# Two projection tiles started over the first 256 tokens ahead of the last token block's turn, the gate's product behind it

## The chip, the cores and the metric

The kernel runs on one core of a Trainium2 chip. The metric is the device time of one execution in microseconds; the kernel before took 1502.77 us as the median of three runs (1499.66 to 1587.22). The engines that matter here are TensorE (PE, with its weight loads PEld), VectorE (DVE), ScalarE (ACT), GpSimd (POOL) and SyncE (SP), whose queue issues the weight transfers.

## The reference

The reference is a decoder trunk of two layers over one sequence of 512 tokens with 1024 channels. Layer 0 mixes tokens with a gated DeltaNet, layer 1 with sparse attention; each is followed by a SwiGLU. What matters here is how one sublayer hands over to the next:

```python
y = gdn_mixer(h, ...)                  # or dsa_mixer, or swiglu: ends in a product with w_out
x = x + (1.0 + ga_m) * rms_norm(y, norm_g[layer, 1])
h = rms_norm(x, norm_g[layer, 2]) * (1.0 + sc_f) + sh_f
gate, up = jnp.split(h @ ffn_w_in[layer], 2, axis=-1)   # the next projection
```

Both norms are over the 1024 channels of one token, so a token's h exists only when its whole y does.

## The kernel before, in words

**Layout.** The 512 tokens are four blocks of 128. The stream x (`x_t`) and each sublayer's output y have tokens on the partitions; the projections want h with channels on the partitions. Between them x is turned on TensorE: a product of 128 x 128 of x with a diagonal matrix that holds 1/rms of each token (`diag`), which transposes and normalizes at once. ACT and DVE then apply scale and shift and cut h into two float32r parts, `h_hi` (rounded) and `h_lo` (the rest). Weights are cut in the same way: ACT makes `w_hi` from the raw weights (`act_split`, L368), DVE makes `w_lo` (`dve_split`, L383). A product is then three: hi x hi, hi x lo, lo x hi.

**Quads and tiles.** Weights come in quads of four tiles (s = 0 to 3) of 128 output channels by 1024 input channels. Tile s is accumulated in PSUM bank s over all 512 tokens, in 8 steps k of 128 channels, 24 products of 512 columns in all (`pe_tile`, L387). SP loads the raw weights of the next quad in two halves (`load_quad`, L330); each half waits until the low parts of two tiles of the quad before are made (`lo_done`). `hi_done` and `lo_done` count split tiles, `tile_done` counts tiles that TensorE has finished.

**The seams.** There are four output stages `pe_out` / `act_out` / `dve_out` / `pool_out` with m = 0 to 3 (DeltaNet's output, the first SwiGLU's, the attention's, the second SwiGLU's). For m = 0, 1 and 2 a projection follows: the first SwiGLU's, the attention's (`dsa_in_pe`), the second SwiGLU's (`ffn_pe`). Such a handover is called a seam here. At its end, for the last block b = 3 (`end`), one chain passes all engines:

- `pe_out` makes y of the block, then turns the block before it (`pe_turn_x`, L693);
- ACT squares y (L794) and DVE scales it by the gate `CB[m]` (L838), adds up the row sum (L841), GpSimd raises it to the power -1/2 (L911, the first root), DVE updates x (L851);
- ACT squares x (L805), DVE adds up (L856), GpSimd takes the second root (L916), DVE makes `diag` (L861);
- TensorE turns the block (L700) into banks 4 to 7, in two groups g of four chunks;
- for the last block ACT writes `h_hi` of group 0 directly from PSUM (`h_last`, L760), DVE writes `h_raw` of group 1, then of group 0 (`h_scale`, L867), ACT rounds group 1 (L766), and DVE makes `h_lo` (`h_low`, L878).

DVE's order after the last block's y is in `dve_out`: split of tile 0 under the first root, `h_scale` of group 1 of block 2 after x, `h_low` of block 2 around the second root, split of tile 1, then the last block's h.

TensorE's first tile of the next quad is `pe_behind_out` (L401): the products with `h_hi` first, as ACT rounds the two groups (`h_rounded`), then those with `h_lo` (`h_made`). Tiles 1 to 3 are plain `pe_tile`.

**The gate's product.** `pe_cb` (L657) multiplies a matrix of ones with a diagonal gate, four products of f32, to spread the gate over all partitions; ACT copies the result into `CB` (`act_cb`, L665). For m = 1 and 2 it stands in TensorE's queue between the turn of block 2 and the turn of block 3 and uses banks 0 and 1. Each engine runs its own instructions in the order written; only semaphores order them against each other.

Of the kernel before, what the change touches and what calls it, by code (L numbers as in the profile page):

```python
# [19 lines left out]
P = 128  # L20
# [58 lines left out]
def build_trunk(nc, x, c, ada_w, ada_b, norm_g, ffn_w_in, ffn_w_out,  # L79
# [4 lines left out]
    DC = D // P  # L84
    NB = S // P
# [19 lines left out]
    Q_FFN = [Q_GDN_OUT + 2, 0]  # L105
# [5 lines left out]
    with ExitStack() as ctx:  # L111
# [178 lines left out]
        def sem(name):  # L290
            if name not in sems:
                sems[name] = ctx.enter_context(nc.semaphore(name))
            return sems[name]
# [13 lines left out]
        def split_tile(w, s, kc=8):  # L307
            return w[:, s, 0:kc * P].rearrange("p (k n) -> p k n", n=P)
# [89 lines left out]
                last = nc.tensor.matmul(out_, lo[:, k, :], r_hi[:, k, :], start=False, stop=k == kc - 1)  # L398
            last.then_inc(tile_done, 1)

        def pe_behind_out(pe, q, m):  # L401

            h = OUT_H[m]
            pe.wait_ge(lo_done, q * 4 + 1)
            hi, lo = split_tile(w_hi, 0), split_tile(w_lo, 0)
            for k in range(DC):
                pe.wait_ge(sem("h_rounded"), 8 * h + 7 + (k >= 4))
                nc.tensor.matmul(ps[:, 0, :], hi[:, k, :], h_hi[:, k, :], start=k == 0, stop=False)
                nc.tensor.matmul(ps[:, 0, :], lo[:, k, :], h_hi[:, k, :], start=False, stop=False)
            for k in range(DC):  # L410
                pe.wait_ge(sem("h_made"), 8 * h + 7 + (k >= 4))
                last = nc.tensor.matmul(ps[:, 0, :], hi[:, k, :], h_lo[:, k, :], start=False, stop=k == DC - 1)
            last.then_inc(tile_done, 1)

        def pe_first_quad(pe, q, r_hi, r_lo, ready, before=None, after=None, between=None):

# [246 lines left out]
            last.then_inc(sem("h_mm"), 1)  # L663

        def act_cb(act, m, bank0):  # L665
            act.wait_ge(sem("h_mm"), DC + 1 if m == 0 else turn_no(m - 1, 3, 1) + 1 if m == 1 else turn_no(m - 1, 2, 1) + 1)
            for j in range(2):
                nc.scalar.activation(CB[m][:, j * S:(j + 1) * S], ps[:, bank0 + j, :], ACT.Copy)\
                    .then_inc(sem("cb_out"), 1)
# [12 lines left out]

        def turn_no(m, b, g):

            return DC + 1 + 9 * m + 2 * b + g + 1 + (1 if m and b == NB - 1 else 0)

        Y_MM = [0, 20, 28, 48]

# [18 lines left out]
        def pe_out(pe, m, q, kc, s_hi, s_lo, ready=None, free=None):  # L707

            late = LATE[m]
            for b in range(NB):  # L710
                if b >= 2 and m % 2:
                    pe.wait_ge(sem("y_added"), 8 * (m // 2) + 2 * (b - 2) + 2)
                elif b >= 2:
                    pe.wait_ge(sem("row_sq"), sq_no(m, b - 2, 0) + 2)
                    pe.wait_ge(sem("y_scaled"), 8 * m + 2 * (b - 2) + 2)
                elif free:
                    free(b)

                def product(k, j):
                    hi, lo = (w_hi[:, k, :], w_lo[:, k, :]) if k < 4 else (late[0][:, k - 4, :], late[1][:, k - 4, :])  # L720
                    cols, toks, to = slice(j * S, (j + 1) * S), slice(b * P, (b + 1) * P), 2 * (b % 2) + j
                    nc.tensor.matmul(ps[:, to, :], s_hi[:, k, toks], hi[:, cols], start=k == 0, stop=False)  # L722
                    nc.tensor.matmul(ps[:, to, :], s_hi[:, k, toks], lo[:, cols], start=False, stop=False)  # L723
                    return nc.tensor.matmul(ps[:, to, :], s_lo[:, k, toks], hi[:, cols], start=False, stop=k == kc - 1)  # L724

                for k in range(4):
                    if b == 0:
                        pe.wait_ge(lo_done, 4 * q + k + 1)
                        if ready:
                            ready(k)  # L730
                    if m == 0 and k == 0:
                        gdn_out_ready(pe, b, k)
                    for j in range(2):
                        last = product(k, j)
                    if b == NB - 1:
                        last.then_inc(tile_done, 1)
                for j in range(2):
                    for k in range(4, kc):
                        if b == 0:
                            per = 4 // (kc - 4)  # L740
                            pe.wait_ge(lo_done, 4 * q + 4 + (k - 4) * per + (per if per == 1 else j + 1))
                            if ready and j == 0:
                                ready(k)
                        if m == 0 and j == 0 and k == 4:
                            gdn_out_ready(pe, b, k)
                        last = product(k, j)
                    last.then_inc(sem("y_mm"), 1)
                if b and m < 3:
                    pe_turn_x(pe, m, b - 1)
            if 1 <= m < 3:  # L750
                pe_cb(pe, m + 1, 0)
            if m < 3:
                pe_turn_x(pe, m, NB - 1)

        def act_out(act, m, nxt):

# [30 lines left out]
            for b in range(NB):  # L787
# [18 lines left out]
                                         accum_out=row_stat[:, 1, b, j:j + 1]).then_inc(sem("row_sq"), 1)  # L806
                if b == NB - 1:
                    h_second(b - 1)
                if m and b == NB - 1:
                    act_cb(act, m + 1, 0)  # L810
                if b == 2:
                    nxt(0)
                    nxt(1)
            if m < 3:
                h_last(NB - 1)
                nxt(2)
                nxt(3)

        def dve_out(dve, m, nxt):
# [31 lines left out]
                    nc.vector.scalar_tensor_tensor(x_half, tmp[:, j, :], row_rinv[:, 0, b:b + 1], x_half,  # L851
                                                   ALU.mult, ALU.add).then_inc(sem("x_made"), 1)

            def root(b, meanwhile=None):
                dve.wait_ge(sem("row_sq"), sq_no(m, b, 1) + 2)
                nc.vector.scalar_tensor_tensor(row_var[:, 1, b:b + 1], row_stat[:, 1, b, 0:1], EPS,  # L856
                                               row_stat[:, 1, b, 1:2], ALU.add, ALU.add).then_inc(sem("row_made"), 1)
                if meanwhile:
                    meanwhile()
                dve.wait_ge(sem("row_root"), row(m, b, 1) + 2)  # L860
                nc.vector.tensor_scalar(diag[:, b, :], ident[:, :], row_rinv[:, 1, b:b + 1], None, ALU.mult)\  # L861
                    .then_inc(sem("x_diag"), 1)
# [28 lines left out]
            if m == 3:  # L891
                scaled(end)
                return
            scaled(end, lambda: nxt(0))
            h_scale(end - 1, 1)
            root(end, lambda: h_low(end - 1, 0))
            h_low(end - 1, 1)
            nxt(1)
            h_scale(end, 1)
            dve.wait_ge(sem("h_rounded"), 8 * OUT_H[m] + 2 * end + 1)  # L900
            h_scale(end, 0)
            h_low(end, 0)
            h_low(end, 1)
            nxt(2)
# [1034 lines left out]
        def ffn_pe(pe, layer, m):  # L1939
            for p in range(3):  # L1940
# [3 lines left out]
                def body(i):  # L1944
                    for s in range(4):
# [7 lines left out]
                            else:  # L1953
                                pe.wait_ge(sem("ffn_silu" if s < 2 else "ffn_mul"), (i + c0) * 2 - 1 + s % 2)

                        if start and s == 0:
                            pe_behind_out(pe, q, 2 * layer)
                        else:
                            pe_tile(pe, i + q, s, h_hi, h_lo, before=free)
                        if layer == 0 and s == 0 and not start:  # L1960
# [105 lines left out]
        def dsa_in_pe(pe, m):  # L2066
            for s in range(4):
                if s == 0:
                    pe_behind_out(pe, Q_DSA, 1)
                else:  # L2070
                    pe_tile(pe, Q_DSA, s, h_hi, h_lo)
                if s == 2:
                    pe_stats(pe, 0, sq_lat[:, 0, :, :], LC)
# [618 lines left out]
```

## Time and profile before

| | |
|---|---|
| median of 3 runs | 1502.77 us (1499.66 to 1587.22) |
| the profiled execution | 1500.31 us |
| its span, first to last instruction | 1498.7 us |
| mean granted TensorE clock | 0.961 |
| TensorE busy | 1385.4 us, 92% |
| VectorE busy | 850.5 us, 57% |
| ScalarE busy | 531.8 us, 35% |
| GpSimd busy | 151.0 us, 10% |

The table is read from the top: the span is what the profiler saw, the time is a little longer than it. The granted clock is the share of 2.4 GHz that TensorE was given. TensorE carries the kernel; the products of the projections (lines 396 to 398) alone are 2808 instructions.

### The profile page before, as it was taken

What the parts mean: (1) busy time and instruction counts of PE and PEld (TensorE: products, weight loads), DVE (VectorE), ACT (ScalarE), POOL (GpSimd) and SP (SyncE); (2) the same over time, 40 slices, a digit from 0 to 9 for tenths busy, and PEclk for the clock granted to TensorE, in tenths of its full rate; (3) what the DMA queues carried; (4) which work ended last, traced back from release to release, by engine and by line L of the source; (5) the groups of instructions that cost most, each with busy time, mean ns of one, the idle gap of its engine ahead of it and who ended that gap; (6) DMA issues with size and microseconds to landing.
All of it is one profiled execution on the core that took longest, in us unless ns stands there. A gap on an engine that the chain in (4) does not pass through costs nothing. (4 is left out here: it accounts for less than half of the span.)

```text
span 1498.7 us, 17980 instructions
## 1 busy us (share of the span) xinstructions
PE 1385.4 (92%) x6983; PEld 1116.6 (75%) x6983; DVE 850.5 (57%) x1412; ACT 531.8 (35%) x953; POOL 151.0 (10%) x155
## 2 busy tenths in 40 slices
PE   5798899899989999999999887699989999999998
PEld 5676777779778878887888765556778888888886
DVE  4768799746555555555555649956453332332335
ACT  2353522345452212221224525476253221221322
POOL 0003330003410000000000102300010000000000
PEclk9899999899999999999999988899999999999999
DMA  9453412110404546455532120200102313322321
GB/s 329 155 169 112 165 61 85 46 68 1 169 28 144 202 159 197 168 168 177 187 141 84 51 56 29 68 18 2 57 29 90 107 61 119 102 84 84 112 84 57
DMA packets 102854, 158.37 MB, mean 106 GB/s; under 512 B 9325, under 2 KB 74106, under 8 KB 102778
## 3 DMA queue, kind: packets, MB, share of 16 engines
q1 hardware_dynamic: 91898, 115.40, 23.5%
q0 software_dynamic: 10880, 41.95, 8.1%
q8 instruction: 49, 0.80, 0.2%
q14 instruction: 27, 0.22, 0.1%
HBM read 155.24 MB, written 2.10 MB: 105 GB/s over the span
## 5 line engine op out<-in xcount | busy, mean ns | idle before, releaser
L396 PE MATMUL ps<-h_hi,w_hi 128*128 128x512 f32 x936 | 378.4, 404 | 0.0
L397 PE MATMUL ps<-h_lo,w_hi 128*128 128x512 f32 x936 | 372.3, 398 | 0.0
L398 PE MATMUL ps<-h_hi,w_lo 128*128 128x512 f32 x936 | 372.3, 398 | 0.0
L380 DVE TENSOR_TENSOR w_lo<-raw,w_hi 128x1024 fp32r<-128x1024 f32 x172 | 210.7, 1232 | 250.1 <-ACT w_hi L374 249.8
L374 ACT ACTIVATE w_hi<-raw 128x1024 fp32r<-128x1024 f32 x180 | 187.7, 1050 | 150.9 <-PE ps L1994 143.0
L396 PEld LDWEIGHTS ps<-h_hi,w_hi 128*128 128x128 f32 x936 | 178.6, 191 | 42.6 <-issue 1.7
L397 PEld LDWEIGHTS ps<-h_lo,w_hi 128*128 128x128 f32 x936 | 178.4, 191 | 42.7 <-issue 1.7
L398 PEld LDWEIGHTS ps<-h_hi,w_lo 128*128 128x128 f32 x936 | 177.8, 190 | 42.5
L462 DVE SCALAR_TENSOR_TENSOR ada_acc<-ada_in,c_act,ada_acc 128x512 f32<-128x512 f32 x147 | 112.9, 768 | 3.9
L1992 PE MATMUL ps<-w_hi,g_hi 128*128 128x512 f32 x256 | 101.6, 397 | 2.6 <-DVE w_lo L380 2.6
L1857 ACT ACTIVATE g_hi<-tmp 128x512 fp32r<-128x512 f32 x44 | 27.8, 632 | 212.0 <-DVE tmp L1892 212.0
L1994 PE MATMUL ps<-w_hi,g_lo 128*128 128x512 f32 x256 | 101.0, 395 | 0.0
L1993 PE MATMUL ps<-w_lo,g_hi 128*128 128x512 f32 x256 | 101.0, 395 | 0.0
L995 DVE SCALAR_TENSOR_TENSOR tmp<-conv_u,conv_t,tmp 128x512 f32<-128x512 f32 x72 | 59.6, 827 | 38.5 <-ACT tmp L989 36.4
L1852 ACT ACTIVATE silu_g<-ps 128x512 f32<-128x512 f32 x44 | 26.3, 597 | 154.1 <-PE ps L398 150.3
L911 POOL TENSOR_TENSOR row_rinv<-row_var,half 128x1 f32<-128x1 f32 x16 | 11.5, 716 | 576.6 <-DVE row_var L841 576.6
L361 POOL DMA_DIRECT2D ada_in<-in_ada_w_dram x40 | 30.5, 761 | 374.5 <-DVE ada_acc L462 365.5
L1892 DVE TENSOR_TENSOR tmp<-silu_g,ps 128x512 f32<-128x512 f32 x44 | 30.3, 688 | 63.5 <-PE ps L398 63.1
L1992 PEld LDWEIGHTS ps<-w_hi,g_hi 128*128 128x128 f32 x256 | 48.1, 188 | 14.7 <-DVE w_lo L380 3.4
L1994 PEld LDWEIGHTS ps<-w_hi,g_lo 128*128 128x128 f32 x256 | 48.1, 188 | 11.5
L1993 PEld LDWEIGHTS ps<-w_lo,g_hi 128*128 128x128 f32 x256 | 48.2, 188 | 11.2
L2441 DVE CUSTOM_DVE_ANT_0 s_m<-ps,mask 128x128 f32<-128x128 f32 (+3 forms) x64 | 29.0, 488 | 26.0 <-PE ps L2341 25.7
(374 smaller groups left out, 2073.3 us busy)
## 6 DMA issues: line engine op xcount, KB each, us to landing
raw<-in_ffn_w_in_dram SPq DMA_DIRECT2D x44, 1024.0 KB, 5.1
ada_in<-in_ada_w_dram POOLq DMA_DIRECT2D x40, 1024.0 KB, 5.7
raw<-in_ffn_w_out_dram SPq DMA_DIRECT2D x20, 1024.0 KB, 5.0
raw<-in_gdn_w_in_dram SPq DMA_DIRECT2D x16, 1024.0 KB, 5.7
ada_in<-in_ada_w_dram SPq DMA_DIRECT2D x4, 1024.0 KB, 7.2
x_t<-in_x_dram SPq DMA_DIRECT2D x2, 2048.0 KB, 9.7
early_slab<-in_ada_w_dram SPq DMA_DIRECT2D x4, 1024.0 KB, 12.3
raw<-in_gdn_w_out_dram SPq DMA_DIRECT2D x4, 1024.0 KB, 4.9
```

Source lines behind the costliest of these rows:

```text
L361: sp.dma_start(slab_place(j)[b][:, :, :], src[b][:, :, bass.ds(jj * 512, 512)])\
L374: nc.scalar.activation(split_tile(w_hi, s, kc) if dst is None else dst(w_hi), raw_tile(s, kc) if src is None else src, ACT.Copy).then_inc( ...
L380: ops.tensor_tensor(lo, raw_tile(s, kc) if src is None else src, f32(hi), ALU.subtract).then_inc(lo_done, 1)
L396: nc.tensor.matmul(out_, hi[:, k, :], r_hi[:, k, :], start=k == 0, stop=False)
L397: nc.tensor.matmul(out_, hi[:, k, :], r_lo[:, k, :], start=False, stop=False)
L398: last = nc.tensor.matmul(out_, lo[:, k, :], r_hi[:, k, :], start=False, stop=k == kc - 1)
L462: ins = nc.vector.scalar_tensor_tensor(ada_acc[:, :], slab_place(j)[b][:, k, :], cc, ada_acc[:, :], ALU.mult, ALU.add)
L995: ins = nc.vector.scalar_tensor_tensor(conv_a[n % 2], conv_u[n % 2][:, j:j + S], conv_t[:, j, channel(n):channel(n) + 1], conv_a[n % 2], A ...
L1892: nc.vector.tensor_tensor(gated[:, s - 2, :], silu_g[:, s - 2, :], ps[:, s, :], ALU.mult)\
L1992: nc.tensor.matmul(ps[:, b, :], g_hi[:, k, toks], hi, start=k == 0, stop=False)
L1993: nc.tensor.matmul(ps[:, b, :], g_hi[:, k, toks], lo, start=False, stop=False)
L1994: last = nc.tensor.matmul(ps[:, b, :], g_lo[:, k, toks], hi, start=False, stop=k == PARTS[p] - 1)
```

## The change

The first tile's function `pe_behind_out` is replaced by two functions that treat tiles 0 and 1 together and split the tokens. `pe_first_tokens` runs the products of `w_hi` with `h_hi` and `h_lo` over tokens 0 to 255; it is called before the last block's turn. `pe_last_tokens` runs, after the turn, the same over tokens 256 to 511, and the products of `w_lo` over all 512. The gate's product moves behind the last turn and from banks 0 and 1 to banks 2 and 3, and ACT's copies of it move behind `h_last`. On DVE, `h_scale` of block 2 moves under the first root, where the split of tile 0 stood; nothing is put under the second root; the split of tile 0 comes after `diag` and that of tile 1 after the last block's `h_scale`. `turn_no` follows the new order of TensorE's signals.

```diff
--- before.py
+++ after.py
@@ -398,19 +398,41 @@
                 last = nc.tensor.matmul(out_, lo[:, k, :], r_hi[:, k, :], start=False, stop=k == kc - 1)
             last.then_inc(tile_done, 1)
 
-        def pe_behind_out(pe, q, m):
-
-            h = OUT_H[m]
-            pe.wait_ge(lo_done, q * 4 + 1)
-            hi, lo = split_tile(w_hi, 0), split_tile(w_lo, 0)
-            for k in range(DC):
-                pe.wait_ge(sem("h_rounded"), 8 * h + 7 + (k >= 4))
-                nc.tensor.matmul(ps[:, 0, :], hi[:, k, :], h_hi[:, k, :], start=k == 0, stop=False)
-                nc.tensor.matmul(ps[:, 0, :], lo[:, k, :], h_hi[:, k, :], start=False, stop=False)
-            for k in range(DC):
-                pe.wait_ge(sem("h_made"), 8 * h + 7 + (k >= 4))
-                last = nc.tensor.matmul(ps[:, 0, :], hi[:, k, :], h_lo[:, k, :], start=False, stop=k == DC - 1)
-            last.then_inc(tile_done, 1)
+        def pe_first_tokens(pe, q):
+
+            part = slice(0, 2 * P)
+            for s in range(2):
+                pe.wait_ge(hi_done, q * 4 + s + 1)
+                hi = split_tile(w_hi, s)
+                for k in range(DC):
+                    nc.tensor.matmul(ps[:, s, part], hi[:, k, :], h_hi[:, k, part], start=k == 0, stop=False,
+                                     skip_group_check=True)
+                    nc.tensor.matmul(ps[:, s, part], hi[:, k, :], h_lo[:, k, part], start=False, stop=False,
+                                     skip_group_check=True)
+
+        def pe_last_tokens(pe, q, m):
+
+            part, h = slice(2 * P, 4 * P), OUT_H[m]
+            for s in range(2):
+                pe.wait_ge(lo_done, q * 4 + s + 1)
+                hi, lo = split_tile(w_hi, s), split_tile(w_lo, s)
+                for k in range(DC):
+                    if s == 0:
+                        pe.wait_ge(sem("h_rounded"), 8 * h + 7 + (k >= 4))
+                    nc.tensor.matmul(ps[:, s, part], hi[:, k, :], h_hi[:, k, part], start=False, stop=False,
+                                     skip_group_check=True)
+                    if k < DC - 1:
+                        nc.tensor.matmul(ps[:, s, :], lo[:, k, :], h_hi[:, k, :], start=False, stop=False,
+                                         skip_group_check=True)
+            for s in range(2):
+                hi, lo = split_tile(w_hi, s), split_tile(w_lo, s)
+                for k in range(DC):
+                    if s == 0:
+                        pe.wait_ge(sem("h_made"), 8 * h + 7 + (k >= 4))
+                    nc.tensor.matmul(ps[:, s, part], hi[:, k, :], h_lo[:, k, part], start=False, stop=False,
+                                     skip_group_check=True)
+                nc.tensor.matmul(ps[:, s, :], lo[:, DC - 1, :], h_hi[:, DC - 1, :], start=False, stop=True,
+                                 skip_group_check=True).then_inc(tile_done, 1)
 
         def pe_first_quad(pe, q, r_hi, r_lo, ready, before=None, after=None, between=None):
 
@@ -663,7 +685,7 @@
             last.then_inc(sem("h_mm"), 1)
 
         def act_cb(act, m, bank0):
-            act.wait_ge(sem("h_mm"), DC + 1 if m == 0 else turn_no(m - 1, 3, 1) + 1 if m == 1 else turn_no(m - 1, 2, 1) + 1)
+            act.wait_ge(sem("h_mm"), DC + 1 if m == 0 else turn_no(m - 1, 3, 1) + 1)
             for j in range(2):
                 nc.scalar.activation(CB[m][:, j * S:(j + 1) * S], ps[:, bank0 + j, :], ACT.Copy)\
                     .then_inc(sem("cb_out"), 1)
@@ -682,7 +704,7 @@
 
         def turn_no(m, b, g):
 
-            return DC + 1 + 9 * m + 2 * b + g + 1 + (1 if m and b == NB - 1 else 0)
+            return DC + 1 + 9 * m + 2 * b + g + 1
 
         Y_MM = [0, 20, 28, 48]
 
@@ -747,10 +769,11 @@
                     last.then_inc(sem("y_mm"), 1)
                 if b and m < 3:
                     pe_turn_x(pe, m, b - 1)
+            if m < 3:
+                pe_first_tokens(pe, (Q_FFN[0], Q_DSA, Q_FFN[1])[m])
+                pe_turn_x(pe, m, NB - 1)
             if 1 <= m < 3:
-                pe_cb(pe, m + 1, 0)
-            if m < 3:
-                pe_turn_x(pe, m, NB - 1)
+                pe_cb(pe, m + 1, 2)
 
         def act_out(act, m, nxt):
 
@@ -806,13 +829,13 @@
                                          accum_out=row_stat[:, 1, b, j:j + 1]).then_inc(sem("row_sq"), 1)
                 if b == NB - 1:
                     h_second(b - 1)
-                if m and b == NB - 1:
-                    act_cb(act, m + 1, 0)
                 if b == 2:
                     nxt(0)
                     nxt(1)
             if m < 3:
                 h_last(NB - 1)
+                if m:
+                    act_cb(act, m + 1, 2)
                 nxt(2)
                 nxt(3)
 
@@ -851,12 +874,10 @@
                     nc.vector.scalar_tensor_tensor(x_half, tmp[:, j, :], row_rinv[:, 0, b:b + 1], x_half,
                                                    ALU.mult, ALU.add).then_inc(sem("x_made"), 1)
 
-            def root(b, meanwhile=None):
+            def root(b):
                 dve.wait_ge(sem("row_sq"), sq_no(m, b, 1) + 2)
                 nc.vector.scalar_tensor_tensor(row_var[:, 1, b:b + 1], row_stat[:, 1, b, 0:1], EPS,
                                                row_stat[:, 1, b, 1:2], ALU.add, ALU.add).then_inc(sem("row_made"), 1)
-                if meanwhile:
-                    meanwhile()
                 dve.wait_ge(sem("row_root"), row(m, b, 1) + 2)
                 nc.vector.tensor_scalar(diag[:, b, :], ident[:, :], row_rinv[:, 1, b:b + 1], None, ALU.mult)\
                     .then_inc(sem("x_diag"), 1)
@@ -891,14 +912,15 @@
             if m == 3:
                 scaled(end)
                 return
-            scaled(end, lambda: nxt(0))
-            h_scale(end - 1, 1)
-            root(end, lambda: h_low(end - 1, 0))
-            h_low(end - 1, 1)
-            nxt(1)
+            scaled(end, lambda: h_scale(end - 1, 1))
+            root(end)
+            nxt(0)
+            h_low(end - 1, 0)
             h_scale(end, 1)
             dve.wait_ge(sem("h_rounded"), 8 * OUT_H[m] + 2 * end + 1)
             h_scale(end, 0)
+            nxt(1)
+            h_low(end - 1, 1)
             h_low(end, 0)
             h_low(end, 1)
             nxt(2)
@@ -1953,8 +1975,9 @@
                             else:
                                 pe.wait_ge(sem("ffn_silu" if s < 2 else "ffn_mul"), (i + c0) * 2 - 1 + s % 2)
 
-                        if start and s == 0:
-                            pe_behind_out(pe, q, 2 * layer)
+                        if start and s < 2:
+                            if s == 0:
+                                pe_last_tokens(pe, q, 2 * layer)
                         else:
                             pe_tile(pe, i + q, s, h_hi, h_lo, before=free)
                         if layer == 0 and s == 0 and not start:
@@ -2066,8 +2089,8 @@
         def dsa_in_pe(pe, m):
             for s in range(4):
                 if s == 0:
-                    pe_behind_out(pe, Q_DSA, 1)
-                else:
+                    pe_last_tokens(pe, Q_DSA, 1)
+                elif s >= 2:
                     pe_tile(pe, Q_DSA, s, h_hi, h_lo)
                 if s == 2:
                     pe_stats(pe, 0, sq_lat[:, 0, :, :], LC)
```

## Rows read from the trace of the kernel before

**Rows 1.** The page, part 1: busy us (share of the span), instructions.

```profile
PE 1385.4 (92%) x6983; PEld 1116.6 (75%) x6983; DVE 850.5 (57%) x1412; ACT 531.8 (35%) x953; POOL 151.0 (10%) x155
```

**Rows 2.** Waits of TensorE: total us, times, longest.

```profile
PE ps L700 <- issue: 13.5, 3, 5.5
```

**Rows 3.** Busy time in four stretches, first seam: each engine, granted clock, DMA.

```profile
437.93:443.42 5.49, 0.01 (x1) 0.04 (x1) 4.62 (x11) 3.35 (x8) 2.19 (x2) 0.79 0.00 0
443.42:447.15 3.73, 3.73 (x17) 3.48 (x17) 1.63 (x2) 1.50 (x4) 0.00 (x0) 0.50 0.22 43
447.15:453.15 6.00, 6.00 (x25) 4.87 (x25) 5.84 (x12) 2.54 (x3) 0.00 (x0) 0.94 0.43 150
453.15:458.70 5.55, 5.55 (x25) 4.53 (x24) 2.74 (x4) 1.55 (x2) 0.00 (x0) 1.00 0.56 189
```

**Rows 4.** The same view, second and third seam: turn of the last block.

```profile
844.48:848.18 3.70, 3.36 (x16) 3.17 (x16) 1.93 (x3) 1.65 (x5) 0.00 (x0) 0.62 0.25 48
1117.74:1121.45 3.71, 3.71 (x16) 3.46 (x17) 1.64 (x2) 1.66 (x5) 0.00 (x0) 0.50 0.13 35
```

**Rows 5.** Timeline of TensorE: start, us; first matmul of each seam's third tile.

```profile
458.74 0.39 PE L396 MATMUL ps<-h_hi,w_hi 128*128 128x512 f32 x1
...
859.48 0.39 PE L396 MATMUL ps<-h_hi,w_hi 128*128 128x512 f32 x1
...
1133.79 0.40 PE L396 MATMUL ps<-h_hi,w_hi 128*128 128x512 f32 x1
```

**Rows 6.** Timeline of all engines, first seam, from the third block's turn.

```profile
435.98 1.95 PE L700 MATMUL ps<-diag,x_t 128*128 128x128 f32 x16
...
439.23 1.41 DVE L851 SCALAR_TENSOR_TENSOR x_t<-tmp,row_rinv,x_t 128x512 f32<-128x512 f32 x2 [0.44 <-POOL row_rinv L911]
...
440.56 1.36 DVE L867 TENSOR_SCALAR h_raw<-ps,coef,mod 128x128 f32<-128x128 f32 x4
...
441.36 0.19 ACT L805 ACTIVATION_READ_ACCUMULATOR tmp<-x_t 128x1 f32 x1
441.84 0.15 DVE L856 SCALAR_TENSOR_TENSOR row_var<-row_stat 128x1 f32<-128x1 f32 x1
...
442.07 0.93 POOL L916 TENSOR_TENSOR row_rinv<-row_var,half 128x1 f32<-128x1 f32 x1 [2.87 <-DVE row_var L856]
443.03 0.29 DVE L861 TENSOR_SCALAR diag<-ident,row_rinv 128x128 f32<-128x128 f32 x1 [0.44 <-POOL row_rinv L916]
...
443.42 3.75 PE L700 MATMUL ps<-diag,x_t 128*128 128x128 f32 x16 [5.49 <-issue]
443.83 1.22 DVE L380 TENSOR_TENSOR w_lo<-raw,w_hi 128x1024 fp32r<-128x1024 f32 x1
...
445.50 1.50 ACT L760 ACTIVATE h_hi<-ps,mod,coef 128x128 fp32r<-128x128 f32 x4 [2.91 <-PE ps L700]
...
447.15 0.77 PE L408 MATMUL ps<-h_hi,w_hi 128*128 128x512 f32 x1
```

**Rows 7.** Timeline, second seam (three rows) and third seam (one row).

```profile
840.29 1.41 DVE L851 SCALAR_TENSOR_TENSOR x_t<-tmp,row_rinv,x_t 128x512 f32<-128x512 f32 x2 [0.44 <-POOL row_rinv L911]
...
842.90 0.15 DVE L856 SCALAR_TENSOR_TENSOR row_var<-row_stat 128x1 f32<-128x1 f32 x1
...
844.48 1.84 PE L700 MATMUL ps<-diag,x_t 128*128 128x128 f32 x7 [4.25 <-issue]
...
1112.10 1.88 PE L662 MATMUL ps<-p_t,ones 128*128 128x512 f32 x4
```

**Rows 8.** Line 911 (GpSimd's first root): ns min/median/max.

```profile
L911 POOL TENSOR_TENSOR row_rinv<-row_var,half x16: 537/541/1457, 404.1 to 1494.3; 128x1 f32<-128x1 f32 x16
```

**Rows 9.** Line 700's weight loads: ns min/median/max.

```profile
L700 PEld LDWEIGHTS ps<-diag,x_t x192: 187/192/338, 410.0 to 1120.9; 128*128 128x128 f32 x192
```

**Rows 10.** Timeline of TensorE: eight one-column products.

```profile
116.17 0.95 PE L1023 MATMUL ps<-ones,tmp 128*128 128x1 f32 x8
```

**Rows 11.** DMA issues, 440 to 470 us: KB each, median us to landing.

```profile
raw<-in_ffn_w_in_dram SPq DMA_DIRECT2D x3, 1024.0 KB, 5.2
```

## The prediction

> **What bounds the kernel now.** I read the share of busy time first: TensorE is busy for 92% of the span [rows 1], so time can only be won where TensorE stands still or runs at its lower clock. The view of waits, asked for TensorE, then names where: line 700, the turn of x, sat behind 13.5 us of idle time in three waits [rows 2]. Those are the three seams the diff touches (m = 0, 1, 2), where the last token block must pass ACT, DVE, GpSimd and the turn before the next projection can begin.
>
> The stretches of the first seam show what one costs. TensorE idles 5.49 us; the granted clock falls, and the turn of the last block runs at 0.50 of full clock (1.2 instead of 2.4 GHz), 3.73 us; tiles 0 and 1 then take 6.00 and 5.55 us [rows 3]. The same 16 products took 1.95 us for the third block at full clock [rows 6]. The last turn is slow in the other seams too (3.70 us at 0.62, 3.71 us at 0.50) [rows 4]. The timeline shows the chain behind the idle time: x updated, both halves squared, the row sum (L856) held until four h_scale instructions end, GpSimd's root at 0.93 us, diag, the turn, ACT's h_hi, first product [rows 6].
>
> **What a half-width product costs.** The change splits the 48 products of 512 columns of tiles 0 and 1 into 64 of 256 columns and 16 of 512. No row has a 256-column product of this kind. A 512-column one costs 5.55 us / 24 = 0.231 us [rows 3]. A turn product (128 columns, f32) costs 1.95/16 = 0.122 us with a weight load of its own [rows 6]; a one-column product costs (0.95 - 0.25)/7 = 0.10 us, 0.25 being an estimated tail [rows 10], so the load alone allows 0.10. Bounds: half of the full product, 0.115, below; the full product's 0.231 above. I take 0.123, next to the turn product, which has just as small a body and as many loads. Columns and thus array work are unchanged; the extra is 64 x (0.123 - 0.1155), 0.5 us in a seam.
>
> **The first tokens in the gap.** 32 half products are 3.94 us. They need the third turn, blocks 0 and 1 of h, and the high halves of two weight tiles that ACT split while the last block was computed; none is late. In seam one they run from 437.93 to 441.87 us. They lie wholly in the gap.
>
> **The chain to the last turn.** DVE does h_scale where it did a split (1.22 us [rows 6]), under the first root. Four h_scale instructions hold DVE for 1.28 us and can start when the third turn ends, 437.97; x would be updated at 439.25 instead of 439.23. So nothing is won there. Afterwards no h_scale stands before L856: it follows ACT's second accumulator read, which ended at 441.55 [rows 6], at 441.59 instead of 441.84. Then the root: 0.93 us of GpSimd with h_low beside it, against a median of 0.541 for the same tiny operation, whose worst was 1.457 [rows 6, 8]. With DVE idle beside it I take 0.54: another 0.38 won. The turn begins at 443.42 - 0.25 - 0.38 = 442.8. TensorE idles 0.9 us instead of 5.5, too little for the clock to fall as it did (the stretch of 5.49 us still averaged 0.79 [rows 3]), and the turn takes 1.95 us, to 444.75.
>
> The trace shows the root slow beside a two-input DVE operation on SBUF. The Trainium skill (SBUF — State Buffer, "SBUF: two separate sides") says the shared port pair is an exclusive lock between DVE with two SBUF inputs and GpSimd; a PSUM-reading h_scale would not take it. By that rule the roots take 0.54; without it they keep 1.46 and 0.93, and the three turns come 0.4 to 0.7 us later.
>
> **The last tokens.** At half clock h_hi began 2.08 us after the turn; at full clock I scale it to 1.08, so 443.9, and the first product follows 1.65 us after [rows 6]: 445.5. Tile 0's part: 8 x (0.123 + 0.231) - 0.231 = 2.60 us, to 448.1. Its second half needs h_rounded of the second group, 446.9, just in time. Tile 1 waits for its low split (lo_done). DVE's new queue is: diag 442.4, split 0 to 443.85, h_low to 444.5, h_scale of the last block after the turn, eight instructions to 447.35, then split 1, to 448.6. TensorE waits 0.6 us. Tile 1's part ends at 451.3, the low parts of h cost 2 x (8 x 0.123 + 0.231) = 2.43 us: 453.75. h_low of the last block ends at 450.6, in time. Before, the third tile began at 458.74 [rows 5]. **Seam one: 5.0 us won.**
>
> **Seam two.** Here split 0 sat before x's update at 840.29 and the third turn was over earlier, so h_scale lets x be updated at 839.92, 0.37 earlier; L856 goes from 842.90 to 842.27 [rows 7], the root saves 0.38: turn at 843.47 instead of 844.48, to 845.42. The first tokens fill 838.5 to 842.45. The gate's product (pe_cb, four products, 1.88 us with its tail [rows 7], 1.72 of cadence) used to lie in the gap for nothing; now it stands behind the turn, and the last tokens can begin at 847.15 rather than 846.2: 0.95 us of it is paid. Split 1 ends at 849.3, no wait. 847.15 + 2.60 + 2.60 + 2.43 = 854.8 against 859.48 [rows 5]: **4.7 us.** ACT's copies of the gate now delay splits 2 and 3 by 1.1 us; split 2's low half is there by 852.5, 2 us before tile 2 wants it.
>
> **Seam three.** As seam one for the chain: turn 1117.74 - 0.62 = 1117.1 to 1119.1, the gate's product to 1120.8, then 7.63 us: 1128.4 against 1133.79 [rows 5]: **5.4 us**, more because the clock had stayed low into tile 0.
>
> **Moved past a queue.** SP loads the next weight pair when split 1 is done. That moves from 445.05 to 448.6 us, 3.6 later; the load lands 5.2 us on [rows 11], 453.8, where ACT wants it at about 453.3. TensorE wants that tile at 453.75 + 11.1 = 464.9, so 0.5 us of ACT delay is covered by some 9 us. GpSimd's queue has only the roots here, now earlier. DVE's other moves are order alone.
>
> **Sum.** 5.0 + 4.7 + 5.4 = 15.1 us. Downstream everything follows TensorE, so I take all of it. Against the profiled execution (1500.31 us, span 1498.7) that is 1485.2. Its time is 2.5 us under the median of the runs shown (1502.77), whose lowest is 1499.66; 1502.77 - 15.1 would be 1487.7. I say 1486.
>
> **Rivals.**
> - *Gain given back (0.15).* The shortened seams meet a new wait: tile 1 on its split in all seams, or the attention layer's first stages, which wait for DVE and ACT chains rather than TensorE. Against it: only one of three seams shows a 0.6 us wait in my sum. If a third to two thirds is lost: 1490 to 1495.
> - *The load is not hidden (0.07), the slower side.* Each half product pays its weight load before it streams 0.107 us. With the load at its recorded 0.19 us [rows 9] it takes 0.30: 64 x 0.177 = 11.3 us in a seam beyond my sum, of which the 0.9 of idle and the 0.6 of wait absorb 1.5; 9.8 - 5.0 = 4.8 us lost in each, 1500.3 + 14.4 = 1515 (0.04). With the load at the 0.10 of the one-column products [rows 10] it takes 0.207: 64 x 0.084 - 1.5 = 3.9 us of each seam's 5.0 are gone, 1497 (0.03). It turns from gain to loss at 0.123 + 6.5/64 = 0.225 us per half product. Against it: turn products, each with a load, run at 0.122 [rows 6].
> - *The whole waste goes (0.05).* TensorE never waits: seam one alone holds 20.8 us from 437.93 to 458.74 for 13.5 us of work, three such gaps about 22 us in all: 1478. It would need the diag to come a microsecond sooner and the last h_hi chain (2.7 us from turn to first product) to vanish; I see no cover for the latter.
> - *The split does nothing (0.02)*: the clock falls all the same in the remaining gap, since 32 small products are thinner work. Then turn and start cost their old 2.5 us again: 1493.
>
> The Trainium skill speaks for that rival (TensorE: Matmul & The Clock Gate, "What overlaps and what doesn't"): a weight load overlaps a running product only when their row groups differ, which no product here does. This trace doesn't agree: full products, each with its own load, follow every 0.231 us, of which 512 columns at 2.4 GHz fill 0.213. By the page's load time of P/1.2, an estimate of 0.107 us, a half product would cost 0.214 and the gain would shrink to about 2 us.
>
> **Chances.** Forecast 0.71, rivals 0.15, 0.07, 0.05, 0.02. The forecast's own range is 1482 to 1490 (half product 0.115 to 0.14, roots 0.54 or slow, which median it is held against). Stretched to the first rival, the clock's and the cheaper load's: 1480 to 1497, which leaves out the 0.04, the 0.05 and the edges of the forecast. A measurement of this kernel tells about 2%, 30 us, from no change. All waste of the three seams is under that, so faster by over 2% gets 0.02; slower by over 2% would need 0.30 us products twice over, 0.02; within 2%: 0.96.
>
> **What would show it.** In the changed trace: 32 products of 256 columns at 0.12 us each in front of the last turn; idle before line 700 about 1 us, three times; granted clock 1.0 through the turn, 1.95 us each; GpSimd's last two roots at 0.54; about 0.6 us of wait before tile 1 in seam one, none in the other two; the next load's issue 3.5 us later with no wait of TensorE for w_lo in the next pair. The prediction is wrong if half products run at over 0.15 us, if the turn stays at 3.7 us, or if the attention layer's waits grow by what the second seam wins.

## The result and the profile after

The changed kernel took 1483.21 us as the median of four runs (1481.28 to 1486.83) against 1501.97 of four for the kernel before; the ratio is 0.9883, 95% interval 0.9856 to 0.991. One execution of the kernel before was in a slower state (1587.22 us) and is left out of the ratio. The forecast was 1486 with 1480 to 1497. A second series of the same kernel on another occasion gave 0.9909 (0.9894 to 0.9924), so the gain is about 18 us by the first series and 14 by the second. The profiled execution took 1483.27 us, its span is 1481.6 us, 17.1 less than before.

The page's part 1 (busy us, share, instructions) and the view of waits of TensorE (total, times, longest), which answer to [rows 1, 2]:

```profile
PE 1373.8 (93%) x7079; PEld 1111.9 (75%) x7079; DVE 850.4 (57%) x1412; ACT 531.3 (36%) x953; POOL 147.6 (10%) x155
```

```profile
PE ps L722 <- issue: 3.3, 3, 1.2
...
PE ps L422 <- ACT h_hi L783: 0.8, 1, 0.8
...
PE ps L422 <- DVE w_lo L380: 0.3, 1, 0.3
```

The turn (now line 722) waits 3.3 us in three seams where it waited 13.5; 96 more products are issued and TensorE is busy 11.6 us less, because fewer of its products run at half clock (mean granted clock 0.971, before 0.961). The stretches of seam one (columns as in [rows 3]: length, busy time of PE, PEld, DVE, ACT, POOL, granted clock, DMA) and the last turn of seams two and three, which answer to [rows 3, 4]:

```profile
439.28:443.08 3.80, 3.80 (x33) 3.59 (x31) 2.82 (x7) 2.89 (x8) 0.35 (x1) 1.00 0.00 0
443.08:444.16 1.08, 0.00 (x0) 0.03 (x1) 0.42 (x3) 0.36 (x1) 0.54 (x1) 1.00 0.00 0
444.16:446.18 2.02, 2.02 (x16) 1.83 (x16) 1.63 (x2) 0.85 (x3) 0.00 (x0) 1.00 0.00 0
446.18:455.09 8.91, 7.85 (x49) 6.96 (x49) 7.85 (x14) 3.78 (x6) 0.00 (x0) 1.00 0.36 120
839.85:841.87 2.02, 2.02 (x17) 2.02 (x18) 1.63 (x2) 0.86 (x3) 0.00 (x0) 1.00 0.00 0
1105.96:1107.98 2.02, 2.02 (x17) 2.02 (x18) 1.64 (x2) 0.85 (x3) 0.00 (x0) 1.00 0.00 0
```

The gap of 5.49 us holds 3.80 us of products and 1.08 of idle time, and the clock is at 1.00 (2.4 GHz) from end to end. The timeline of seam one shows the chain, row by row against [rows 6]:

```profile
439.24 0.28 PE L410 MATMUL ps<-h_lo,w_hi 128*128 128x256 f32 x1
...
440.61 1.41 DVE L874 SCALAR_TENSOR_TENSOR x_t<-tmp,row_rinv,x_t 128x512 f32<-128x512 f32 x2
...
442.80 0.28 PE L410 MATMUL ps<-h_lo,w_hi 128*128 128x256 f32 x1
...
442.96 0.16 DVE L879 SCALAR_TENSOR_TENSOR row_var<-row_stat 128x1 f32<-128x1 f32 x1 [0.94 <-ACT tmp L828]
443.19 0.54 POOL L938 TENSOR_TENSOR row_rinv<-row_var,half 128x1 f32<-128x1 f32 x1 [3.56 <-DVE row_var L879]
443.77 0.28 DVE L882 TENSOR_SCALAR diag<-ident,row_rinv 128x128 f32<-128x128 f32 x1 [0.66 <-POOL row_rinv L938]
...
444.16 2.02 PE L722 MATMUL ps<-diag,x_t 128*128 128x128 f32 x16 [1.08 <-issue]
...
446.98 0.36 PE L422 MATMUL ps<-h_hi,w_hi 128*128 128x256 f32 x1 [0.80 <-ACT h_hi L783]
...
448.78 1.22 DVE L380 TENSOR_TENSOR w_lo<-raw,w_hi 128x1024 fp32r<-128x1024 f32 x1
...
450.05 0.39 PE L422 MATMUL ps<-h_hi,w_hi 128*128 128x256 f32 x1 [0.26 <-DVE w_lo L380]
```

The third tile's first product, in the three seams, against [rows 5]:

```profile
455.09 0.39 PE L396 MATMUL ps<-h_hi,w_hi 128*128 128x512 f32 x1
...
850.92 0.39 PE L396 MATMUL ps<-h_hi,w_hi 128*128 128x512 f32 x1
...
1117.06 0.39 PE L396 MATMUL ps<-h_hi,w_hi 128*128 128x512 f32 x1
```

**Where the 17.1 us are.** I cut each trace at the end of the third turn and at the third tile's first product of each seam. "Seam" below is the stretch between the two:

| trace | seam 1 | seam 2 | seam 3 | their sum | between 2 and 3 |
|---|---|---|---|---|---|
| before | 20.8 | 21.0 | 21.5 | 63.3 | 252.8 |
| changed | 15.8 | 16.0 | 16.0 | 47.8 | 250.2 |

The seams give 15.5 us. The stage between seams two and three, whose code is the same, gives 2.6; the stretch ahead of seam one took 1.4 us more, what follows seam three 0.3 less. The 1.4 us are not the change's either: when the changed kernel ran once more, that stretch took 437.3 us, against 439.3 here and 437.9 before. The difference lies in waits for VectorE inside DeltaNet (`qkv` 6.8 us against 5.2 in the kernel before and in the repeat, `w_quarter` 4.8 against 3.2). The stage between seams one and two is equal (379.8 in both).

### The profile page after: what moved, and what is told of

Its sections match the earlier page's. It is cut to its first block and busy times, and to the rows that moved or that the text cites. A ratio compares the mean times of both kernels' runs of the same rounds, so it can differ in the third digit from the quotient of the medians.

```text
span 1481.6 us, 18172 instructions
## 1 busy us (share of the span) xinstructions
PE 1373.8 (93%) x7079; PEld 1111.9 (75%) x7079; DVE 850.4 (57%) x1412; ACT 531.3 (36%) x953; POOL 147.6 (10%) x155
## 5 line engine op out<-in xcount | busy, mean ns | idle before, releaser
L396 PE MATMUL ps<-h_hi,w_hi 128*128 128x512 f32 x912 | 367.7, 403 | 0.0
L397 PE MATMUL ps<-h_lo,w_hi 128*128 128x512 f32 x912 | 361.6, 396 | 0.0
L398 PE MATMUL ps<-h_hi,w_lo 128*128 128x512 f32 x912 | 361.4, 396 | 0.0
L397 PEld LDWEIGHTS ps<-h_lo,w_hi 128*128 128x128 f32 x912 | 173.3, 190 | 41.1 <-issue 1.7
L396 PEld LDWEIGHTS ps<-h_hi,w_hi 128*128 128x128 f32 x912 | 173.3, 190 | 41.0 <-issue 1.7
L398 PEld LDWEIGHTS ps<-h_hi,w_lo 128*128 128x128 f32 x912 | 172.7, 189 | 41.0
```

Source lines behind the costliest of these rows:

```text
L396: nc.tensor.matmul(out_, hi[:, k, :], r_hi[:, k, :], start=k == 0, stop=False)
L397: nc.tensor.matmul(out_, hi[:, k, :], r_lo[:, k, :], start=False, stop=False)
```

## The experiments

Each was compared with the kernel before on the same chip. The first four take the change apart.

**DVE's new order alone.** The kernel before with:

```diff
-            scaled(end, lambda: nxt(0))
-            h_scale(end - 1, 1)
-            root(end, lambda: h_low(end - 1, 0))
-            h_low(end - 1, 1)
-            nxt(1)
+            scaled(end, lambda: h_scale(end - 1, 1))
+            root(end)
+            nxt(0)
+            h_low(end - 1, 0)
             h_scale(end, 1)
             dve.wait_ge(sem("h_rounded"), 8 * OUT_H[m] + 2 * end + 1)
             h_scale(end, 0)
+            nxt(1)
+            h_low(end - 1, 1)
             h_low(end, 0)
```

> The kernel before with DVE's new order alone. TensorE's order is the old one, with no work in the gap. My theory (the gain is TensorE's idle time and its low clock): the last turn starts 0.6, 1.0 and 0.6 us sooner in the three seams, its clock still falls, so the stretch from the end of the third turn to the third tile goes from 20.8, 21.0 and 21.5 us to about 20.2, 20.0 and 20.9: 2.2 us won, 0.15%. Rival (DVE's order, with the free port under the roots, is what pays): 5 us or more won, and a turn at full clock.

Measured: ratio 0.9982 (0.9969 to 0.9995). Seams of 21.2, 21.2 and 19.5 us: 1.4 won in all, not 2.2, and spread otherwise than I said. TensorE's rows with idle time, in seams one, two and three:

```profile
442.65 3.75 PE L700 MATMUL ps<-diag,x_t 128*128 128x128 f32 x16 [4.87 <-issue]
451.47 2.13 PE L412 MATMUL ps<-h_lo,w_hi 128*128 128x512 f32 x8 [0.47 <-DVE h_lo L878]
...
843.74 3.65 PE L700 MATMUL ps<-diag,x_t 128*128 128x128 f32 x16 [3.24 <-issue]
...
852.46 2.12 PE L412 MATMUL ps<-h_lo,w_hi 128*128 128x512 f32 x8 [0.81 <-DVE h_lo L878]
...
1115.04 2.02 PE L700 MATMUL ps<-diag,x_t 128*128 128x128 f32 x16 [3.15 <-issue]
```

The idle time shrinks by the forecast 0.6 to 1.0 us. But the old TensorE order then waits for DVE, which has put the split of tile 1 ahead of h_low: 0.47 us of idle time in seam one, 0.81 in seam two and 0.32 in seam three. I had not counted that wait. With it seam one is 0.4 us longer where it should have won 0.6, and seam two 0.2 us longer where it should have won 1.0. In seam three the turn ran at full clock after 3.15 us of idle time, in seam two at half after 3.24; the 2.0 us won in seam three are mostly the clock's. The rival, 5 us or more from DVE's order, is out.

**TensorE's new order alone.** The changed kernel with the hunk above undone; `root` again takes work to do under the root.

> The changed kernel with DVE's old order: splits of tiles 0 and 1 and h_low under the roots. TensorE's new order and the gate's product behind the turn stay. My theory: each last turn starts 0.6, 1.0 and 0.6 us later than in the changed kernel, tile 1's wait for its split in seam one goes, so 2.0 us are lost of the 17: stretches of 16.2, 17.0 and 16.6 us against 15.8, 16.0 and 16.0, about 1485 us. Rival (DVE's order is what pays): 5 us or more lost; GpSimd's last two roots are slow again (0.9 to 1.5 us) in both.

Measured: 0.9922 (0.9898 to 0.9945); seams 15.9, 18.7 and 16.6, together 3.3 us more than the changed kernel against 2.0 expected. Seams one and three came as I said or better; seam two lost 2.7 and not 1.0. Its stretches, idle and turn:

```profile
837.96:840.14 2.18, 0.00 (x1) 0.03 (x1) 1.74 (x7) 0.95 (x3) 0.93 (x1) 1.00 0.00 0
840.14:843.10 2.96, 2.96 (x17) 2.96 (x18) 1.64 (x2) 1.51 (x4) 0.00 (x0) 0.65 0.05 8
```

A gap of 2.18 us leaves the clock at 1.00 within the gap and at 0.65 over the turn behind it, and the gate's product started at half clock too. The turn began 1.0 us later than in the changed kernel (5.97 us behind the third turn's end, against 4.97), as expected; the other 1.7 us of seam two's loss come behind its start and go with the lower clock. So of the 3.3 us that DVE's order is worth, about 1.6 are its timing and 1.7 the clock that a smaller gap kept. GpSimd's roots are slow again (line 934 is the first root; ns min/median/max), against 0.59 at most in the changed kernel (line 933):

```profile
L934 POOL TENSOR_TENSOR row_rinv<-row_var,half x16: 538/542/1457, 404.7 to 1480.5; 128x1 f32<-128x1 f32 x16
```

```profile
L933 POOL TENSOR_TENSOR row_rinv<-row_var,half x16: 540/540/585, 405.5 to 1477.2; 128x1 f32<-128x1 f32 x16
```

**The clock by itself.** The kernel before with unused products ahead of the last turn:

```diff
+                pe.wait_ge(sem("y_scaled"), 8 * m + 2 * (NB - 1) + 2)
+                pe.wait_ge(sem("row_sq"), sq_no(m, NB - 1, 0) + 2)
+                for s in range(2):
+                    pe.wait_ge(hi_done, (Q_FFN[0], Q_DSA, Q_FFN[1])[m] * 4 + s + 1)
+                    for k in range(DC if m == 0 else 6):
+                        for part_of in (h_hi, h_lo):
+                            nc.tensor.matmul(ps[:, 2 + s, 0:2 * P], split_tile(w_hi, s)[:, k, :],
+                                             part_of[:, k, 0:2 * P], start=k == 0, stop=False,
+                                             skip_group_check=True)
                 pe_turn_x(pe, m, NB - 1)
```

> The kernel before with work that nobody uses in the gap ahead of the last turn: 32 (seam one) and 24 (seams two and three) products of 256 columns into banks 2 and 3, which are overwritten later. Nothing is moved. It takes the clock by itself. My theory: the turn runs at full clock (1.95 us), h_hi begins 1.1 us after it and not 2.1, tile 0 starts at full clock: 1.45, 1.1 and 2.0 us won in the seams, 4.6 in all, about 1496 us; the rest of the 15.5 is the work moved into the gap. Rival (the clock costs nothing that counts, h_hi's chain sets it all): no change within 1 us.

Measured: 0.9964 (0.9953 to 0.9975); seams 19.5, 20.0 and 19.5, 4.2 us won where 4.6 were expected. Seam one:

```profile
445.91 2.02 PE L700 MATMUL ps<-diag,x_t 128*128 128x128 f32 x16 [1.69 <-issue]
448.72 0.47 PE L408 MATMUL ps<-h_hi,w_hi 128*128 128x512 f32 x1 [0.80 <-ACT h_hi L769]
```

Of the 1.7 us that the turn is shorter, 0.80 comes back as a wait for ACT's h_hi; 0.3 us more are won in tile 0, which starts at full clock. In all the clock pays 1.3, 1.0 and 2.0 us in the three seams. The rest of the gain, 15.5 - 4.2 = 11.3 us, is close to three times the 3.80 us of first tokens, which are now useful work. That it is so close is partly chance, as smaller terms nearly cancel: the turns begin 0.6, 1.0 and 0.6 us sooner, and against that stand the gate's product (0.75 us, twice) and tile 1's wait (0.4 us).

**The first tokens behind the turn.** The changed kernel with two lines exchanged:

```diff
-                pe_first_tokens(pe, (Q_FFN[0], Q_DSA, Q_FFN[1])[m])
                 pe_turn_x(pe, m, NB - 1)
+                pe_first_tokens(pe, (Q_FFN[0], Q_DSA, Q_FFN[1])[m])
```

> The changed kernel with the first tokens' products behind the last turn and not ahead of it; same products, same DVE order. My theory (their place is what pays, not the split of the tiles): TensorE idles 4.9 us again in each seam, the turn takes about 3.7, the first tokens 4 to 6 us behind it, where they cover only the 0.8 us wait for h_hi; stretches of about 21, 23 and 23 us, 1500 to 1504 us in all, no better than before. Rival (two tiles treated together pay by themselves, since the chain of h_hi and h_lo is covered by them wherever they stand): 8 us or more of the 17 remain.

Measured: 0.9995 (0.9984 to 1.0006); seams 20.5, 21.8 and 22.3, in all 1.2 us longer than before. All turns are back at half clock; seam one:

```profile
443.42 3.75 PE L722 MATMUL ps<-diag,x_t 128*128 128x128 f32 x16 [4.87 <-issue]
```

Seams two and three also carry the gate's product behind the turn here (1.7 us), which the kernel before had in the gap. Seam one has none and is the clean comparison: 20.5 us against 20.8. So the same products in the same number, with DVE's new order, win 0.3 us behind the turn, where the changed kernel wins 5.0 with them ahead of it. Their place is what pays.

**The changed kernel and the kernel before once more**, for the size and for the stage between seams two and three.

> The changed kernel once more, unaltered, beside the others on one chip. Settles the size and what of the 17 us lies outside the seams. My theory: the three stretches come out at 15.8, 16.0 and 16.0 us again (15.5 us under before), the stage between seams two and three at 250.1 us as in four of the five traces so far that have other seams, and the ratio at 0.9895 (1484.5 us). Rival (the new order of seam two also shortens the attention layer behind it by 2.6 us): the ratio stays at 0.988 and every trace of the kernel before has 252.8 us there.

> The kernel before once more, for its trace. The stage from the third tile of the attention projection to the end of seam three's third turn took 252.8 us in its first trace, 250.2 in the changed kernel. My theory (a matter of the granted clock in that stage, which differs from execution to execution): about 250 us here too. Rival (the change causes it): 252.8 us again.

Measured: the changed kernel 0.9909 (0.9894 to 0.9924), seams 15.8, 16.1 and 16.0, the stage 250.1 us. The kernel before: seams 20.8, 21.0 and 21.5, the stage 252.8 us again. My theory that it would come out near 250 fell: both kernels repeat their value in their two traces. But the rival doesn't hold either. The stage took 250.2, 250.0 and 250.1 us in the kernels with DVE's order alone, with the filler and with the first tokens behind the turn, the first two of which keep TensorE's old order of products; and 251.5 us in the kernel with TensorE's order alone and 253.0 and 251.7 us in the two below, which have the new one. Between the kernel before and the changed one it differs in two places, and both are at a lower granted clock. Stretches from the first to the last of the latent query's products and over the first 30 products of the output projection, before, then changed:

```profile
881.90:916.73 34.83, 29.36 (x125) 22.66 (x126) 25.03 (x64) 16.01 (x32) 6.86 (x4) 0.86 0.09 31
1059.64:1069.24 9.60, 9.60 (x30) 7.62 (x30) 7.06 (x7) 0.63 (x1) 0.00 (x0) 0.68 0.42 138
```

```profile
873.36:906.90 33.54, 28.55 (x125) 21.85 (x126) 25.05 (x64) 16.02 (x32) 6.88 (x4) 0.90 0.09 32
1049.67:1058.07 8.40, 8.40 (x30) 6.72 (x30) 7.06 (x7) 0.63 (x1) 0.00 (x0) 0.80 0.35 107
```

The same work is 1.3 us longer in the first place and 1.2 in the second at the lower clock. What decides when the clock rises there, and why a kernel repeats its value, stays open; 2.6 us of the measured gain are of this kind and can't be credited to the change's reasons. The ratios of the single experiments hold such microseconds too, so what a change is worth is read from the seams.

The times themselves say how far one execution can be trusted. The five executions of the repeat took 1481.24 and 1482.84 us at a mean granted clock of 0.971 and 0.970, and 1487.18 to 1487.81 us at 0.966 and 0.967. The kernel before, in the series beside the first four experiments, lies between 1496.93 us at 0.964 and 1503.01 us at 0.962. The two profiles of the changed kernel are of executions of 1483.27 and 1481.24 us; none of the four above 1486 us has a trace, so what those do otherwise is not shown.

**The gate's product in two halves.** The changed kernel; `pe_cb` takes the halves it is to make and signals with the second. A half is one call of its loop, which stands as two products in the trace:

```diff
                 pe_first_tokens(pe, (Q_FFN[0], Q_DSA, Q_FFN[1])[m])
+                if m:
+                    pe.wait_ge(sem("y_scaled"), 8 * m + 2 * (NB - 1) + 2)
+                    pe.wait_ge(sem("row_sq"), sq_no(m, NB - 1, 0) + 2)
+                    pe_cb(pe, m + 1, 2, (0,))
                 pe_turn_x(pe, m, NB - 1)
             if 1 <= m < 3:
-                pe_cb(pe, m + 1, 2)
+                pe_cb(pe, m + 1, 2, (1,))
```

> The changed kernel with the gate's product cut in two: its first two products (one PSUM bank) go ahead of the last turn, behind the first tokens, the other two stay behind the turn. My theory: in seams two and three TensorE's 1.1 us of idle time ahead of the turn takes the first half (0.86 us) for nothing, and the second half fits in the 0.8 us that TensorE waits for h_hi; the last tokens begin 0.8 us sooner, of which a 0.2 us wait for tile 1's split is given back: stretches of 15.8, 15.4 and 15.3, 1.3 us less than the changed kernel. Rival (h_hi's chain or ACT's copies already set the start): no change, 16.0 and 16.0.

Measured: 0.9903 (0.9887 to 0.9918); seams 15.8, 15.9 and 15.8, 0.3 us less than the changed kernel, not 1.3. Seam two, around the last turn and at tile 1:

```profile
840.03 2.02 PE L723 MATMUL ps<-diag,x_t 128*128 128x128 f32 x16 [0.31 <-issue]
...
844.65 1.21 DVE L380 TENSOR_TENSOR w_lo<-raw,w_hi 128x1024 fp32r<-128x1024 f32 x1
...
845.91 0.39 PE L422 MATMUL ps<-h_hi,w_hi 128*128 128x256 f32 x1 [0.26 <-DVE w_lo L380]
```

The first half did go into the idle time, which fell from 1.17 to 0.31 us with the turn as early as before. Tile 0's part starts 0.8 us sooner (7.8 us behind the third turn's end, against about 8.55). But tile 1 then waits for its split, as in seam one. The wait that I put at 0.2 us is 0.4: tile 0's last product starts at 845.37 and would be followed after 0.12, the split ends at 844.65 + 1.21 = 845.86, and the next product starts at 845.91. The first products of the two parts, which now follow a pause, also take 0.19 and 0.23 us to the next instead of 0.12. Together 0.6 of the 0.8 us come back.

**The split of tile 1 earlier.** On top of the halves:

```diff
             nxt(0)
-            h_low(end - 1, 0)
+            nxt(1)
             h_scale(end, 1)
             dve.wait_ge(sem("h_rounded"), 8 * OUT_H[m] + 2 * end + 1)
             h_scale(end, 0)
-            nxt(1)
+            h_low(end - 1, 0)
             h_low(end - 1, 1)
```

> As the kernel with the gate's product in two halves, and on DVE the split of tile 1 directly behind that of tile 0, ahead of the turn's h_scale, with h_low of block 2 last. My theory: the wait for tile 1's split (0.3 us in seam one, then also in the other two) goes, and h_scale starts 0.1 to 0.2 us later: stretches of 15.6, 15.2 and 15.1, 1.9 us less than the changed kernel. Rival (h_scale delayed holds up the second half of h_hi and so the products behind it): 0.3 us longer in each seam than with the halves alone.

Measured: 0.9887 (0.9872 to 0.9902), 1483.33 us; seams 15.3, 15.4 and 15.3, in all 1.9 us less than the changed kernel, as expected. DVE in seam two:

```profile
840.81 2.35 DVE L380 TENSOR_TENSOR w_lo<-raw,w_hi 128x1024 fp32r<-128x1024 f32 x2
...
843.08 2.64 DVE L893 TENSOR_SCALAR h_raw<-ps,coef,mod 128x128 f32<-128x128 f32 x8
```

The two splits run 0.1 us past the turn's end at 843.02, and the h_scale behind them starts 0.06 us after it, hardly later than in the changed kernel (0.04). TensorE no longer waits for w_lo in any seam. By its seams this is the shortest version. Its whole trace (1482.4 us) isn't shorter than the changed kernel's two (1481.6 and 1479.6), as the stretch ahead of seam one took 441.0 us and the attention stage 251.7; and in the times it can't be told from the changed kernel beside it, whose interval (0.9894 to 0.9924) overlaps.

## Why the prediction was right

**The half-width product.** Forecast 0.123 us, between 0.115 and 0.231. Thirty of them lie between the rows at 439.24 and 442.80: 0.119 us each. The rival of the load that isn't hidden (1515 or 1497 us) is out. The Trainium skill's rule that I set beside it (TensorE: Matmul & The Clock Gate, "What overlaps and what doesn't"), that a load overlaps a running product only with other row groups, does not hold here: each product has its own 128-column load. One bound was a little low: the eight one-column products of line 1023 start 0.11 us apart behind the first, not 0.10, so with a load of its own a product of 256 columns costs hardly more than one of a single column.

**Seam one** came out term by term, counted from the third turn's end: first tokens 3.80 us (3.94), x updated after 1.33 (1.32), turn after 4.88 (4.87), its length 2.02 (1.95), first product of the last tokens after 7.70 (7.6), third tile after 15.81 (15.82). Tile 1's wait for its split was real: tile 0's last product starts at 449.51 and would be followed after 0.12, the next starts at 450.05, so 0.4 us are lost. The forecast said 0.6, though its own times (448.1 and 448.6) give 0.5.

**Seams two and three**: 4.9 and 5.6 us won against 4.7 and 5.4. The term that was a little too dear is the gate's product behind the turn. I charged 0.95 us; the real cost in seam two is about 0.75, as its four products end near 841.71 + 4 x 0.43 = 843.4 and the start it delays was 842.67 (turn's end at 841.87 plus 0.80, the wait for h_hi in seam one). The half products behind it, at 0.119 instead of 0.123 us, give another 0.1. The halves then showed that this start was worth little by itself, as tile 1's split came due right behind it.

**The roots** took 0.54 us each, as the Trainium skill's rule on the shared port pair (SBUF — State Buffer, "SBUF: two separate sides") has it, and 1.46 and 0.93 where DVE's old order stood. Undoing that order cost 3.3 us, though, about half of it through the clock and not through the roots.

**The clock** held at 1.00 in all three seams after 1.08 to 1.17 us of idle time. The filler puts its share at 4.2 of 15.5 us.

**The moved load** was issued at 450.18, which is 3.6 us later than before if the 1.35 us that the trace runs late are taken off; TensorE had no wait for w_lo in the pair that follows. What I had said of it holds.

**The sum** was 15.1 us; the seams gave 15.5. What the sum didn't have are the 2.6 us in the attention layer and the 1.4 lost ahead of seam one, both places where no instruction changed. The mechanism and the seams are what the prediction had right; that the whole time came within 3 us of 1486 is in part luck, since executions of this kernel spread over 6 us (1481.24 to 1487.81). The first rival, a gain given back by the attention layer, did not come: TensorE's waits there add up to 35.4 us, against 34.9 before.

## What to carry to other kernels

Ask of every gap on the bounding engine what part of the next stage depends only on data that is already there: here half the tokens of the next projection were ready by the third turn's end, 4.9 us ahead of the last turn, and the seams won 15.5 us with their products in the gap and nothing with the same products behind it. A gap can cost more than its length, when the engine restarts at half clock: in one seam a turn 1.0 us later cost 2.7 us, in another one 0.6 us sooner won 2.0; where the clock held all the same, 0.6 us later cost 0.6 in one seam and almost nothing in another, whose wait for tile 1's split went with it. When one start is made earlier, look at once for the next input that comes due (tile 1's split), or the gain stays on paper.

## What I had not expected of the hardware

The length of an idle gap alone didn't tell whether the clock fell. In the kernel with DVE's order alone, these are gap and turn of seam two and of seam three:

```profile
840.50:843.74 3.24, 0.00 (x1) 0.04 (x1) 1.64 (x5) 2.72 (x8) 0.54 (x1) 1.00 0.00 0
843.74:847.38 3.64, 3.64 (x16) 3.45 (x16) 1.63 (x2) 1.76 (x5) 0.00 (x0) 0.53 0.00 0
1111.88:1115.04 3.16, 0.01 (x2) 0.04 (x1) 1.56 (x5) 2.69 (x7) 0.54 (x1) 1.00 0.00 0
1115.04:1117.06 2.02, 2.02 (x16) 1.83 (x16) 1.63 (x2) 1.11 (x4) 0.00 (x0) 1.00 0.00 0
```

Both gaps were at 1.00 to their end; 3.24 us was followed by a turn at 0.53, 3.16 us by one at 1.00, and in the kernel with TensorE's order alone 2.18 us by one at 0.65, while 1.69 us in that kernel's other two seams kept it full. The fall after 2.18 us came when TensorE had been back at work for 0.9 us; these are the two parts of that turn:

```profile
840.14:841.01 0.87, 0.87 (x8) 0.87 (x9) 0.87 (x2) 0.00 (x0) 0.00 (x0) 1.00 0.00 0
841.01:843.10 2.09, 2.09 (x12) 2.09 (x11) 0.77 (x1) 1.51 (x4) 0.00 (x0) 0.50 0.07 11
```

Of the gaps ahead of the last turns in all ten traces, those of 0.2 to 1.7 us kept the clock, those of 3.8 to 5.5 us were followed by a turn at 0.50 to 0.62, and between them both happened. What decides between them is not shown.
